# Two stacked blocks on one core: the first modulation in four slabs of columns, and the value groups accumulated in fp32 while it loads

## What is computed

```python
cond = jax.nn.silu(c)
mod = cond @ w_ada[l] + b_ada[l]                  # 2048 x 6144
shift, scale, gate = jnp.split(mod, 3, axis=-1)
h = rms_norm(x, norm_g[l]) * (1.0 + scale[:, None, :]) + shift[:, None, :]
z = h @ w_in[l]                                   # 2048 x 7184
u_a, v_a, g_a, q_b, k_b, v_b, g_b, f_b = jnp.split(z, pts, axis=-1)
y_a = chunked_spatial_gating(gelu(u_a), gelu(v_a), ...) * silu(g_a)
y_b = forgetting_attention(q_b, k_b, v_b, f_b, b_f[l]) * silu(g_b)
x = x + gate[:, None, :] * (jnp.concatenate([y_a, y_b], -1) @ w_out[l])
return rms_norm(x, final_g)
```

## Time and profile before

| | us |
|---|---|
| median of 3 runs (3304.21 to 3306.54) | 3305.11 |
| span of the profiled execution, first to last instruction | 3300.8 |
| TensorE busy | 2958.6 (90%) |
| VectorE busy | 1836.1 (56%) |
| ScalarE busy | 1066.8 (32%) |
| DMA queue, share of 16 engines | 41.4% |

### The profile page before, as it was taken

How to read it: one execution, slowest core, us unless ns; L and a number is a source line. 1 busy time by engine, 2 the same in 40 slices (tenths; PEclk the granted TensorE clock), 3 DMA queues, 4 the chain that set the end, 5 groups by cost and what they waited for, 6 DMA issues and landing times.

```text
span 3300.8 us, 39727 instructions
## 1 busy us (share of the span) xinstructions
PE 2958.6 (90%) x13275; PEld 2348.7 (71%) x13275; DVE 1836.1 (56%) x2889; ACT 1066.8 (32%) x1714; POOL 3.9 (0%) x10
## 2 busy tenths in 40 slices
PE   3499999989999969599999999999899698999996
PEld 2377887666777847378878687787788477787784
DVE  6857763444577454355437456473866666324443
ACT  2332222333332254322233435342322421223324
POOL 0000000000000000000000000000000000000000
PEclk8699999999999979799999999999999799999997
DMA  9766552222356436165522222224566263332331
GB/s 370 272 197 189 185 165 68 64 64 64 108 166 208 166 101 216 62 216 191 167 83 77 70 65 94 70 76 138 181 204 205 75 218 121 91 100 89 111 114 51
DMA packets 219344, 451.54 MB, mean 137 GB/s; under 512 B 23752, under 2 KB 29338, under 8 KB 214860
## 3 DMA queue, kind: packets, MB, share of 16 engines
q1 hardware_dynamic: 219212, 449.82, 41.4%
HBM read 422.47 MB, written 27.30 MB: 136 GB/s over the span
## 4 chain that ended last, share of the span: by engine, by line
PE 80%; DVE 6%; ACT 4%; issue 3%; DVEq 2%; DMA 2%; ACTq 1%; SPq 1%; PEldq 0%; PEld 0%
PE ps L1006 19%; PE ps L1008 19%; PE ps L1007 19%; PE ps L1015 3%; PE ps L1016 3%; PE ps L1017 3%; PE ps L1348 3%; PE ps L985 1%; PE ps L1058 1%; PE ps L1213 1%; PE ps L1221 1%; DMA a_raw<-in_w_ada 1%; DVE acc L1593 1%; PE ps L1381 1%; PE ps L1378 1%
## 5 line engine op out<-in xcount | busy, mean ns | idle before, releaser
L1006 PE MATMUL ps<-op_hi,w_hi 128*128 128x512 f32 (+2 forms) x2928 | 1186.0, 405 | 105.8 <-DVE op_lo L1505 47.3
L1008 PE MATMUL ps<-op_hi,w_lo 128*128 128x512 f32 (+2 forms) x2928 | 1158.4, 396 | 0.0
L1007 PE MATMUL ps<-op_lo,w_hi 128*128 128x512 f32 (+2 forms) x2928 | 1158.0, 396 | 0.0
L1006 PEld LDWEIGHTS ps<-op_hi,w_hi 128*128 128x128 f32 (+1 forms) x2928 | 562.9, 192 | 251.5 <-issue 58.3
L1457 DVE TENSOR_TENSOR w_lo<-w_raw,w_hi 128x512 fp32r<-128x512 f32 x496 | 342.3, 692 | 596.9 <-ACT w_hi L570 592.2
L1008 PEld LDWEIGHTS ps<-op_hi,w_lo 128*128 128x128 f32 (+1 forms) x2928 | 561.8, 192 | 122.5
L1007 PEld LDWEIGHTS ps<-op_lo,w_hi 128*128 128x128 f32 (+1 forms) x2928 | 563.8, 193 | 112.8 <-issue 1.7
L570 ACT ACTIVATE w_hi<-w_raw 128x512 fp32r<-128x512 f32 x496 | 313.0, 632 | 1022.1 <-PE ps L1008 849.1
L1419 DVE SCALAR_TENSOR_TENSOR acc<-a_raw,vec,acc 128x512 f32<-128x512 f32 x576 | 419.7, 747 | 22.5 <-DMA a_raw<-in_w_ada 22.0
L1405 DVE TENSOR_TENSOR w_lo<-w_raw,w_hi 128x512 fp32r<-128x512 f32 (+2 forms) x240 | 145.6, 610 | 207.7 <-ACT w_hi L546 206.8
L546 ACT ACTIVATE w_hi<-w_raw 128x512 fp32r<-128x512 f32 (+2 forms) x240 | 134.8, 565 | 366.8 <-PE ps L1008 285.6
(11 more groups left out here) (208 smaller groups left out, 2245.0 us busy)
## 6 DMA issues: line engine op xcount, KB each, us to landing
a_raw<-in_w_ada SPq DMA_DIRECT2D x224, 512.0 KB, 4.0
w_raw<-in_w_in_e SPq DMA_DIRECT2D x160, 512.0 KB, 4.3
w_raw<-in_w_in SPq DMA_DIRECT2D x112, 512.0 KB, 4.8
arena<-in_w_ada SPq DMA_DIRECT2D x64, 512.0 KB, 8.0
w_raw<-in_w_in_o SPq DMA_DIRECT2D x64, 512.0 KB, 4.2
w_raw<-in_w_out SPq DMA_DIRECT2D x32, 512.0 KB, 5.0
w_raw<-in_w_out_e SPq DMA_DIRECT2D x32, 512.0 KB, 5.0
w_raw<-in_w_out_o SPq DMA_DIRECT2D x32, 512.0 KB, 3.6
```

Of the source, the lines that this page charges most:

```text
L1006: mm(dst, hi[:, cols], B.op_hi[:, k, 0:tok], start=first, stop=False)
L1007: mm(dst, hi[:, cols], B.op_lo[:, k, 0:tok], start=False, stop=False)
L1008: last = mm(dst, lo[:, cols], B.op_hi[:, k, 0:tok], start=False, stop=last_t)
```

## The change

The load stage now comes in four **slabs**. Slab s has columns 512s to 512s+511 of shift and of scale; a chunk is one K-tile of both (two rows of 2 KB for each partition where it was one of 4 KB), and the ring has 6. x is loaded ahead of all chunks. A slab gives the shift and scale of four K-tiles of the operand. VectorE normalises and modulates these four (`slab_normed`, `slab_modulated`, with `norm_g` put into the scale) while it accumulates the next slab, and TensorE multiplies them at once with the value weights of those K-tiles: both value groups, four banks each, in plain fp32 (one matmul for a position, no split). The value weights come in 16 blocks of two K-tiles of one group, through the slots of `w_raw`; those of the last slab's second half lie in `a_raw`. Bank 7 is needed for reductions too, so what would be its sum is kept in the arena (`park`). The operand is still split for the later groups (`slab_low`). The value groups have no parts any more: f, q, k and v have one each, and ck has two. x is stored after f's stream. The part of v's second group is reduced just before the mixing.

```diff
     for n, x in enumerate(g):
         x["kc"] = kc
-        kc += x["kt"]
+        kc += x["kt"] if x["name"] != "va" else 0
...
-    for start, count in ((first["va"], 8), (first["gb"], 5), (first["ck"], 1), (first["r"], 6),
+    for start, count in ((first["f"], 7), (first["gb"], 5), (first["ck"], 2), (first["r"], 6),
...
+START_RING, SLABS, SLAB = 6, 4, 4
+VALUE_AT = (6, 9, 12, 15)
...
+def va_block(b):
+    slab, m = divmod(b, 4)
+    slot = m if slab < SLABS - 1 or m < 2 else RAW + m - 2
+    fills = sum(va_slot(x) == slot for x in range(b + 1))
+    return m % 2, SLAB * slab + 2 * (m // 2), slot, fills
...
+    def value_weights(b):
+        g, kt, slot, fills = va_block(b)
+        if slot < RAW and b >= RAW:
+            sp.wait_ge(sem("va_used"), b - RAW + 1)
+        if slot >= RAW:
+            sp.wait_ge(sem("masks_made"), 1)
...
+    for n in range(SLABS * KT):
+        slab, kt = divmod(n, KT)
+        if n >= START_RING:
+            sp.wait_ge(sem("acc_step"), n - START_RING + 1)
+        sp.dma_start(ring[:, n % START_RING, :, :], w_ada[:, kt, 0:2, slab * GC:(slab + 1) * GC])\
+            .then_inc(B.start_in[n % START_RING], 16)
...
+        if kt in VALUE_AT:
+            value_weights(4 * slab + VALUE_AT.index(kt))
...
-    sp.wait_ge(sem("x_turned"), KT)
-    sp.dma_start(B.x_sp, B.Y[:, :, :]).then_inc(sem("spilled"), 16)
...
+        if not o and m < 2:
+            sp.wait_ge(sem("va_used"), 4 * SLABS)
...
+        if name == "f":
+            sp.wait_ge(sem("x_turned"), KT)
+            sp.dma_start(B.x_sp, B.Y[:, :, :]).then_inc(sem("spilled"), 16)
             sp.wait_ge(sem("op_tile"), KT)
+            sp.wait_ge(sem("va_used"), 4 * SLABS)
...
+    def reduce_slab(slab):
+        pe.wait_ge(sem("acc_step"), KT * (slab + 1))
+        if slab:
+            pe.wait_ge(sem("parked"), slab)
+        else:
+            pe.wait_ge(sem("variance"), 1)
+        reduce_parts(slab % 2, ps[:, 7, :]).then_inc(sem("start_summed"), 1)
...
+    reduce_slab(0)
+    for slab in range(SLABS):
+        for b in (4 * slab + 1, 4 * slab + 3):
+            for k in range(2):
+                pe.wait_ge(sem("modulated"), va_block(b)[1] + k + 1)
+                last = value_product(slab, b, k, 3)
+        last.then_inc(sem("park_summed"), 1)
+        for b in range(4 * slab, 4 * slab + 4):
+            for k in range(2):
+                if slab < SLABS - 1 and b % 4 == 3 and k == 1:
+                    reduce_slab(slab + 1)
+                for j in range(3 if b % 2 else 4):
+                    last = value_product(slab, b, k, j)
+            last.then_inc(sem("va_used"), 1)
...
+    for n in range(SLABS * KT):
+        slab, kt = divmod(n, KT)
+        accumulate(n)
...
+        else:
+            if n == KT:
+                dve.wait_ge(sem("deviation"), 1)
+                slab_normed(0)
+            if kt == 1:
+                slab_columns(slab - 1)
+                slab_modulated(slab - 1)
+            if kt in (4, 5, 6, 7):
+                slab_low(slab - 1, kt - 4)
+            if kt == 8:
+                park(slab - 1)
+            if kt == 15:
+                slab_normed(slab)
```

More of the change, by code:

```diff
@@ L264, in sync_program @@
     sp.dma_start(B.const[:, :], A["const"]).then_inc(sem("const_in"), 16)
[L267 to L276, removed]
+    sp.dma_start(at(AT_X_TOK, NT, D), A["x"][0].rearrange("(n p) d -> p n d", p=P)).then_inc(sem("x_in"), 16)
@@ new lines, in sync_program @@
+    ring = at(AT_START, START_RING, 2, GC)
+    w_ada = A["w_ada"][0].rearrange("(k p) (h n) -> p k h n", p=P, h=3)
+    def value_weights(b):
[4 more added lines that the diff above has]
+            sp.wait_ge(sem("masks_made"), 1)
+        dst = B.w_raw[:, slot, :, :] if slot < RAW else B.a_raw[:, slot - RAW, :, :]
+        sp.dma_start(dst, B.weight(GROUPS[g])[:, kt:kt + 2, GROUPS[g]["col"]:GROUPS[g]["col"] + GC])\
+            .then_inc(B.va_in[slot], 16)
@@ L660, in scalar_program @@
         Act(Y[:, t, :], ps[:, 1 + t % 4, :], ACT.Copy).then_inc(sem("x_turned"), 1)
-    norm(0, 1)
-    from_mod(0, m=0)
+    norm(0, 0)
+    for slab in range(SLABS):
+        for t in range(SLAB):
+            k = SLAB * slab + t
+            act.wait_ge(sem("modulated"), k + 1)
+            Act(B.op_hi[:, k, :], slab_input(B, slab)[:, t, :], ACT.Copy).then_inc(sem("op_high"), 1)
+    for c in range(4):
+        high_tile(c, GROUPS[FIRST["f"]]["width"])
     for n, g in enumerate(GROUPS):
@@ new lines, in slab_normed, with slab_modulated @@
+    def slab_normed(slab):
+        if slab >= 2:
+            dve.wait_ge(sem("va_used"), 4 * (slab - 1))
+            dve.wait_ge(sem("op_high"), SLAB * (slab - 1))
+        V.tensor_tensor(slab_input(B, slab), Y[:, SLAB * slab:SLAB * slab + SLAB, :],
+                        at(AT_RSTD_X, 1, S).to_broadcast([P, SLAB, S]), ALU.mult)
+        V.drain()
+    def slab_modulated(slab):
+        x = slab_input(B, slab)
+        for t in range(SLAB):
+            k = SLAB * slab + t
+            V.tensor_scalar(x[:, t, :], x[:, t, :], B.mod[:, 16 + k:17 + k], B.mod[:, k:k + 1],
+                            ALU.mult, ALU.add).then_inc(sem("modulated"), 1)
@@ new lines, in slab_low, with park @@
+    def slab_low(slab, t):
+        k = SLAB * slab + t
+        dve.wait_ge(sem("op_high"), k + 1)
+        dve.wait_ge(sem("modulated"), k + 1)
+        split_lo(k, slab_input(B, slab)[:, t, :])
+    def park(slab):
+        dve.wait_ge(sem("park_summed"), slab + 1)
+        x = at(AT_PARK, S)
+        if slab == 0:
+            last = V.tensor_copy(x, ps[:, 7, :])
+        else:
+            last = V.tensor_tensor(x, x, ps[:, 7, :], ALU.add)
+        V.drain().then_inc(sem("parked"), 1)
+    dve.wait_ge(sem("vec_ready"), 1)
@@ L1610, in scaled @@
+    slab_columns(SLABS - 1)
+    slab_modulated(SLABS - 1)
+    for t in range(SLAB):
+        slab_low(SLABS - 1, t)
+    park(SLABS - 1)
     def scaled(m):
```

165 lines of the change are left out of this document (101 added, 64 removed).

## The result

The changed kernel takes 3346.66 us (median of 4 runs, 3346.56 to 3350.25), against 3304.66 us (3302.37 to 3306.54) for the kernel before in the same comparison: a ratio of 1.0129, 95% interval 1.0115 to 1.0144. It is slower, as forecast, but by 42 us and not by 18; 3346.66 lies 3.7 us outside the range of 3293 to 3343.

What follows compares the result with a forecast made beforehand. Loading bounds the first 134 us, then TensorE; the value groups' overlap is eaten. 13.9 (f and q) + 1.9 (mixing) + 2.9 (ck) = +18.7 on the 3300.8 span, plus 4.3 to the median: 3323 us, range 3293 to 3343.

Steps and rivals of the forecast that it cites:

- two stops of SyncE's queue in a slab: Slab cycles: waiting value blocks stop loading twice, leaving TensorE idle 6.9 us before the reduction and 9.3 before the next slab.
- the spill: Group f: x's 4 MB store stands ahead of f's last three pairs, so q's tile 4 starts 13.9 us later.
- A slab's cycle: Value groups: start at 59.0, two cycles of 99.8 us together, then 39.0 and 27.5, ending at 225.3.
- last three positions 3.0: Slab cycle, behind the reduction: the last three product positions take TensorE 3.0 us, from 37.5 to 40.5.
- A chunk in 1.31 us, 400 GB/s: Load stage: each 512 KB chunk, in 2 KB rows, moves at 400 GB/s and takes 1.31 us.
- 17.6 + 4.1 + 8 x 1.31: Cycle from slab 2 to 3: chunks 10 to 15 wait until 17.6; loading and accumulation end at 32.2 us.
- Mixing: Before the mixing: reducing the part of v's second group at full clock, behind an existing 2.5 us wait, adds 1.9 us.
- ck: Group ck's second half: a 1.84 us reduction in cv and 1 us of stall add 2.9; bound 0 to +4.
- The offset: Whole kernel: the median of the runs lies 4.3 us above the profiled span, added to reach the forecast time.
- Slower still: Load stage: 2 KB rows move at only 325 GB/s, +13 us, giving 3336 to 3340 us; chance 0.13.
- No change: Slab gaps or group f: clock hardly falls, or x's store is not in f's way; 3303 to 3311 us; chance 0.17.
- Faster, 3279, loading never held: Slab cycles: the ring of six chunks carries VectorE over SyncE's waits, a cycle takes 31.4 us; 3279 us; chance 0.10.

Runs made afterwards that it cites:

- the second profile: The changed kernel run once more without any edit, for another profile; one run, 3345.66 us.
- warm: Changed kernel with eight extra fp32 products, results unused, ahead of the reductions of slabs 1 to 3; 3335.7 us.
- rows4k: Changed kernel with each chunk reading 1024 adjacent columns of w_ada in 4 KB rows instead of two 2 KB rows; 3340.68 us.
- mix: Changed kernel with the last three modulation pairs of v's second half issued one behind each of ua's first three weight pairs; 3341.84 us.
- ring6: Changed kernel with six slots for the value blocks instead of four, each block waiting for the block six before; 3286.85 us.
- ring5: Changed kernel with five slots for the value blocks instead of four, each block waiting for the block five before; 3304.62 us.
- all: Changed kernel with ring6, mix, x stored in slab 1, and f's first modulation pairs waiting for value block 12, not 16; 3272.3 us.
- allwarm: The kernel all with eight extra unused fp32 products ahead of the first reduction and four behind it; 3276.79 us.

## Why the prediction was wrong in size

**Right.** The direction; the mechanism, two stops of SyncE's queue in a slab; the price of a product position (27.5 us a slab); and the spill. The third value block of slab 1 went out at 24.47 us from the slab's start (24.5 forecast), the idle time ahead of the next slab was 9.6 (9.3), and q's tile 4 came 50.7 us after the last value block (50.5). What stalls f there is in VectorE's timeline:

```profile
271.44 0.75 DVE L1521 SCALAR_TENSOR_TENSOR acc<-a_raw,vec,acc 128x512 f32<-128x512 f32 x1 [14.77 <-DMA a_raw<-in_w_ada]
```

**The step that failed: "A slab's cycle" and its sum, value groups that end at 225.3.** They end at 238.87, 13.6 later (240.65 and 15.4 in the second profile): slab 0 by 1.7 (60.67 for 59.0), the cycles by 3.8 and 2.7 (53.7 and 52.7 for 49.9), and the stretch from slab 2's start to the end by 5.4 (71.9 for 66.5), of which 3.3 lie ahead of the last reduction (35.5 for 32.2) and 2.1 behind it. Two terms of it were too small, and a queue was taken for empty:
- *"last three positions 3.0"*. They took 5.47 (99.33 to 104.80), which is 2.5 of the first cycle's 3.8. I had taken the clock to be nearly back by then. The stretches from 95 to 104 show 0.50 throughout: the clock was not back after the 16 narrow matmuls of one column each. Behind the last reduction it stayed at half still longer, into slab 3's products (0.50 in the stretch from 206 to 211). With work ahead of the reductions, `warm` has the value groups end 12.4 us earlier; my terms held 6.5 for what it takes away (three reductions of 3.58 for 1.84, and three times 3.0 for 2.6).
- *A chunk in 1.31 us, 400 GB/s.* While the queue was full, rows of 2 KB moved at 369 GB/s, 1.42 us a chunk:

```profile
182.00:196.00 14.00, 11.75 (x28) 4.94 (x26) 8.23 (x8) 0.00 (x0) 0.00 (x0) 1.00 1.03 369
```

  The 340 from 180 to 200 above is a mean with both ends of the burst in it, and not the rate. Slab 0's last chunks moved at 385 (40 to 60). So 400 was too high, but nearer than my lower bound, 325. `rows4k` gives some 4 us.
- *"17.6 + 4.1 + 8 x 1.31", slab 2's loading.* It counts from the wait that ends at 17.6 as if nothing were in flight. But that issue came at 184.34, and a value block and three chunks had been issued from 179.19 on, four transfers that take 5.7 us at 1.42 each, so that some were still to land. That sum should have been a chain of transfers from the first of them. The experiments do not price this term by itself.

The Trainium skill, "DMA: Bandwidth & Descriptors", section "Where 436 GB/s comes from", has a core's HBM reads bound near 358 GB/s. The 385 GB/s from 40 to 60 and the 369 from 182 to 196 speak against it again, and `ring6` has 366, 349 and 359 in three stretches of 20 us, so the rows show no bound at that figure.

My working also has slips that change little: 87.08 us over 384 products is 0.2268 and not 0.2266, 35.8 + 3.0 is 38.8 and not 39.0, and slab 0's terms add up to 58.7 and not 59.0.

**Mixing, 1.9 forecast, 7.0 to 9.3 measured.** I priced the reduction at full clock and put it behind an existing wait of 2.5 us. I had not looked at what the three pairs of the part do to the queue: they wait for slots ahead of ua's first weights. It is the mechanism I had found for the slabs, overlooked at a second place. `mix` takes back 4.8.

**ck, 2.9 forecast, 3.5 to 4.5 measured**, within its bound of 4 more. No experiment undid ck's second part.

**Not forecast: 2.5 to 2.9 us from gb to the final norm**, in unchanged code. It stays open.

**The offset.** I called the 4.3 us from the span to the median what starting and ending take. In the later runs an execution's time lies some 1.8 us above its span (the kernel before: 3303.8 on a span of 3302.0; the changed kernel: 3350.25 on 3348.4). So the profiled execution of the kernel before took some 3302.6 us and was 2.5 under the median. The name was wrong, but the sum does not suffer: the 18.7 us are simply added to the median, and it is they that fell short, by 23.3 us of the 42.0.

**The rivals.** "Slower still", 3336 to 3340, came nearest, 6.7 us short, and its cause holds for a small part; the rate of 369 GB/s and the 6.0 us that `rows4k` gained speak against 13 us from the rows. "No change" is refuted: the clock fell in every gap of a slab's cycle, and the spill was in f's way. "Faster, 3279, loading never held" did not happen, yet it describes what the same products do once the queue lets them: 29.25 us a cycle in `ring6`.

## What to carry to other kernels

Before loads are put between other loads in one in-order queue, follow the chain from each issue that waits: which product must be finished, what does that product wait for, and how far ahead of this issue in the queue do the loads stand that it needs? Where they stand just ahead, nothing can be loaded while they are consumed, and the loads behind start from an empty queue. The sign in the profile is a DMA share of 0.3 in a stage that should be full of loading. Here one more slot (a wait one block further back) was worth 42 us and a second one 18, of which 4.5 are the late weights of f in `ring5`: with the same products and the same bytes the kernel is 1.3% slower than before, equal to it, or 0.5% faster. A stall priced on one queue should be looked for at every other place where the change puts a waiting issue ahead of other work, and a reduction by narrow matmuls behind an idle time should be priced, with what follows it, at the half clock.

## What was not expected of the hardware

- The clock stayed at 1.2 GHz through 16 matmuls of 128x1 and the six records of 128x512 behind them, 95.89 to 104.8, after 8.21 us without work; with eight 128x512 products ahead, the same 16 took 1.95 us and not 3.57.
- DMA with TensorE full and rows of 2 KB moved 349 to 366 GB/s over stretches of 20 us in `ring6`, and 369 in the changed kernel from 182 to 196. With 4 KB rows the kernel before has 387 to 408. What makes the rate differ among stretches of 2 KB rows was not tried.
- Two profiles of one program differ by 3.7 us in the stretch with the heads of the linear attention, and `all` and `allwarm` by 4.5 in the median with the same start of f and of q, their runs overlapping: differences under some 5 us between kernels need the rows of the place they are claimed for.
